# Transposing the mixer input before its scale and shift are known, and scaling it in place

## The chip, the cores and the metric

One core of one Trainium2 chip. The metric is the device time of one execution in microseconds (us); a kernel's time is the median of several executions. TensorE (PE), VectorE (DVE), ScalarE (ACT) and GpSimd (POOL) compute; SP, ACT and POOL issue DMA transfers, each on a queue of its own (in the profile q1 is SP's, q10 ACT's, q0 POOL's).

## The reference, cut to what matters

One trunk layer of width 2048 over 128 context tokens and 512 latent tokens. A modulation vector per token group comes from a matrix product with the conditioning vectors; its first two parts shift and scale the normalised input of the mixer:

```python
xs = x_sample + grid_pos_embed(x_sample.shape[1], x_sample.dtype)[None]
mod = (silu(cond) @ w_mod + b_mod)            # six parts of 2048: sh1, sc1, gt1, sh2, sc2, gt2
h = rmsnorm(x, norm_mix) * (1 + sc1) + sh1    # both groups, each with its own sh1, sc1
proj = h @ w_in                               # q, k, v first
qkv = silu(short_conv(qkv, conv_w))
```

After this come a DeltaNet scan, a gated MLP, the merge, the output projection and a retrieval over 16384 experts. Everything is float32.

## The kernel before, in words

The work around the change is at the start of the program, in three blocks. A block ends when all five engines have reached its end, and one follows the other (`build`, L2713 to L2718).

**`modulation` (L428).** SP loads 32 tiles of `w_mod` of 1 MB each into a ring of four slots (L451; `load_tile`, L232, waits until the tile four places earlier has been used), and behind them the first four `w_qkv` tiles. PE multiplies each tile by the conditioning vectors (`modulate`, L246); four tiles make one of eight groups. ACT copies a group's result out of PSUM (`copy`, L476), and PE turns it into columns (`turn`, L504). Between these, PE forms the row part of the positions (`encode`, L513, behind every third tile from 4 to 25), DVE adds it and the column part to the four latent blocks x[1] to x[4] (L550 to L555), ACT takes the sum of squares of each block (L489), DVE the reciprocal root and five normalised blocks (L561). The normalised blocks 1 to 4 have buffers of their own; x[1] to x[4] hold the sums of input and position, which ACT writes to DRAM (`x_rows`, four transfers of 1 MB, L498) behind the copy of group 6, for use much later. At the end DVE makes `shift1` and `scale1` (L565 to L570).

**`mixer_input` (L574).** For each of 16 slices of 128 features PE transposes five 128x128 squares (L604), DVE scales and shifts the latent 512 columns (L585) and ACT the context's 128 (L593), each out of PSUM into `l.h` and `c.h`. POOL issues the first three `w_mod` tiles of the next stage (`mod_load`, L285), and DVE waits for `x_rows` (L587), since the memory of x[1] to x[4] is written next.

**`qkv` for the context (L613).** 24 tiles of `w_qkv`: PE projects (`project`, L239, 16 products of 128x128x128 each), DVE convolves (L729 to L735), ACT applies SiLU and a square (L804, L807), PE sums the squares of tile n-1 behind the projection of tile n (`norm_sum`, L660), and behind every tile PE does one more `w_mod` tile (`mod_tile`, L254), whose loads POOL issues (`mod_feed`, L297). SP first loads `w_gates` and `c_masks` (1.4 MB together, L636, L638), then `w_qkv` tiles from the fifth on, each when the ring slot four places back is free.

Of the kernel before, what the change touches and what calls it, by code (L numbers as in the profile page):

```python
# [9 lines left out]
ACT = mybir.ActivationFunctionType  # L10
# [63 lines left out]
def after(e, sem, n):  # L74

    if n > 0:
        e.wait_ge(sem, n)
# [350 lines left out]
def modulation(nc, t, a):  # L428
# [5 lines left out]
    normed = x[0:1] + [t.m[:, o:o + D] for o in (DD + D, DD + 2 * D, DD + 3 * D, E + D)]  # L434
    t.normed = normed
    row_enc = t.m[0:2, BG:BG + (NB - 1) * D // 2].rearrange("p (b n) -> p b n", b=NB - 1)
# [9 lines left out]
    with nc.Block() as block:  # L446
# [10 lines left out]
        def _(act):  # L457
# [36 lines left out]
            for n in range(NB, groups):  # L494
                copy(n)
                if n == groups - 2:
                    for b in range(1, NB):
                        act.dma_start(t.x_rows[b], x[b]).then_inc(t.x_spilled, 16)  # L498
# [4 lines left out]
        def _(pe):  # L503
# [9 lines left out]
            def encode(i):  # L513
# [3 lines left out]
                else:  # L517
                    pe.wait_ge(row_read, i)
                pe.matmul(t.ps[:, 3, :], which, row_enc[:, i // 2, i % 2 * COL:(i % 2 + 1) * COL],
                          start=True, stop=True).then_inc(row_ps, 1)  # L520

            pe.wait_ge(small_done, 2)
            pe.wait_ge(sel_step, 3)
            for n in range(groups):

                after(pe, copied, n - 1)
                for kq in range(4):
                    tile_full(pe, t, 4 * n + kq)
                    mm = modulate(pe, t.ps[:, n % 2, :], t, 4 * kq, tile_slot(t, 4 * n + kq), kq == 0, kq == 3)
                    mm.then_inc(t.tile_done, 1)  # L530
                    if 4 <= 4 * n + kq < 28 and (4 * n + kq) % 3 == 1:
                        encode((4 * n + kq) // 3 - 1)
                if n:
                    turn(n - 1)
# [3 lines left out]
        def _(dve):  # L538
# [22 lines left out]
            for b in range(NB):  # L561
                nc.vector.tensor_scalar(normed[b], x[b], inv[:, b:b + 1], None, ALU.mult).then_inc(xn_done, 1)
            dve.wait_ge(turned, groups)
            dve.wait_ge(t.x_in, 16 * 8)
            for i, out in ((0, t.shift1), (1, t.scale1)):  # L565
# [4 lines left out]
                                           op0=ALU.add, op1=ALU.mult).then_inc(t.init, 1)  # L570
    t.tiles += tiles


def mixer_input(nc, t, a):  # L574

    c, l = t.group[:2]
    x = t.normed
    turned, lat_read, ctx_read = (t.sem("mi_" + n) for n in ("turned", "lat_read", "ctx_read"))
    with nc.Block() as block:  # L579
        @block.vector  # L580
        def _(dve):
            for k in range(KD):

                dve.wait_ge(turned, k + 1)
                nc.vector.tensor_scalar(l.h[:, k, :], t.ps[:, 2 * (k % 4), :], t.scale1[:, k, 1:2], t.shift1[:, k, 1:2],  # L585
                                        ALU.mult, ALU.add).then_inc(lat_read, 1)
            dve.wait_ge(t.x_spilled, 16 * (NB - 1))  # L587

        @block.scalar
        def _(act):  # L590
            for k in range(KD):
                act.wait_ge(turned, k + 1)
                nc.scalar.activation(c.h[:, k, :], t.ps[:, 2 * (k % 4) + 1, 0:P], ACT.Identity,  # L593
                                     bias=t.shift1[:, k, 0:1], scale=t.scale1[:, k, 0:1]).then_inc(ctx_read, 1)

        @block.tensor
        def _(pe):
            for k in range(KD):

                after(pe, lat_read, k - 3)  # L600
                after(pe, ctx_read, k - 3)
                for b in range(NB):
                    out = t.ps[:, 2 * (k % 4), (b - 1) * P:b * P] if b else t.ps[:, 2 * (k % 4) + 1, 0:P]
                    mm = pe.transpose(out, x[b][:, k * P:(k + 1) * P], t.ident[:])  # L604
                mm.then_inc(turned, 1)

        @block.gpsimd
        def _(pool):
            for m in range(3):
                mod_load(pool, t, a, m)  # L610


def qkv(nc, t, a, g, block):  # L613
# [13 lines left out]
                                   "qk_done", "gates_ps", "gates"))  # L627
    first_staged = t.sem("qk_first_staged")
    tiles, normed = 3 * H, 2 * H
# [30 lines left out]
    def _(pe):  # L660
# [39 lines left out]
        for n in range(tiles):  # L700

            after(pe, psum_read, n - 3)
            tile_full(pe, t, n)
            project(pe, t.ps[:, n % 4, 0:nt], tile_slot(t, n), h).then_inc(t.tile_done, 1)
            if 1 <= n <= normed:
# [15 lines left out]
    def _(dve):  # L721
# [23 lines left out]
        def last_product():  # L745

            dve.wait_ge(gates, 9)
            nc.vector.tensor_tensor(beg, beg, beta, ALU.mult).then_inc(gates, 1)

        for n in range(tiles):  # L750
            conv(n)
# [31 lines left out]
    def _(act):  # L783
# [12 lines left out]
        for n in range(tiles):  # L796
# [5 lines left out]
            if n < normed:  # L802
                after(act, qk_done, n - 1)
                nc.scalar.activation(s[n % 2], y[n % 2], ACT.Silu).then_inc(silu_done, 1)  # L804
                act.wait_ge(silu_done, n + 1)
                after(act, norm_ps, n)
                nc.scalar.activation(sq, s[n % 2], ACT.Square).then_inc(sq_done, 1)  # L807
            else:
                nc.scalar.activation(heads[:, n, :], y[n % 2], ACT.Silu).then_inc(silu_done, 1)
            gelu_rows(act, nc, t, behind[n])  # L810
            if n == q + 6 and not ctx:
# [1884 lines left out]
def build(nc, a):  # L2696
    with ExitStack() as ctx:
# [16 lines left out]
        retire()  # L2714
        mixer_input(nc, t, a)
        retire()
        with nc.Block() as block:
# [140 lines left out]
```

## Time and profile before

| what | us |
|---|---|
| median of three executions | 4789.78 |
| lowest and highest of them | 4781.29, 4797.11 |
| profiled execution, first to last instruction (its span) | 4786.7 |
| end of `modulation`, first transpose of `mixer_input` | 111.7, 111.84 |
| first product of the context's projection | 130.30 |

Of the profiled execution the span is what is known of its own time; it lies 3.1 us under the median of the three. Times in the rows below count from the first instruction. A row of the timeline has start, busy time, engine, line, operation, output<-input, shape and count, and in brackets the engine's idle time before it and what ended that. A row of the windows has, for a stretch, its length, the busy time of each engine with its count of instructions in brackets, then the granted share of TensorE's clock, the busy share of the 16 DMA engines and the GB/s they moved.

### The profile page before, as it was taken

What the parts mean: (1) busy time and instruction counts of PE and PEld (TensorE: products, weight loads), DVE (VectorE), ACT (ScalarE), POOL (GpSimd) and SP (SyncE); (2) the same over time, 40 slices, a digit from 0 to 9 for tenths busy, and PEclk for the clock granted to TensorE, in tenths of its full rate; (3) what the DMA queues carried; (4) which work ended last, traced back from release to release, by engine and by line L of the source; (5) the groups of instructions that cost most, each with busy time, mean ns of one, the idle gap of its engine ahead of it and who ended that gap; (6) DMA issues with size and microseconds to landing.
All of it is one profiled execution on the core that took longest, in us unless ns stands there. A gap on an engine that the chain in (4) does not pass through costs nothing.

```text
span 4786.7 us, 61495 instructions
## 1 busy us (share of the span) xinstructions
PE 4559.0 (95%) x25813; PEld 3365.2 (70%) x25813; DVE 3043.3 (64%) x4399; ACT 579.6 (12%) x1080; POOL 1656.3 (35%) x1110
## 2 busy tenths in 40 slices
PE   6989999999888999899999998999999999999997
PEld 2776346444888544347555545699999999999997
DVE  1451006888877777417777667988865557886556
ACT  1531001441222100000000001110000000000000
POOL 0131001674655554210544443433432332322221
PEclk8999999999999999999999999999999999999998
DMA  9919898997322998997999997579999999999998
GB/s 400 383 63 368 314 347 321 384 393 288 110 83 90 361 390 352 421 369 270 408 420 420 411 413 300 220 294 420 418 417 421 405 406 419 417 417 419 404 420 326
DMA packets 237328, 1663.47 MB, mean 348 GB/s; under 512 B 28231, under 2 KB 32729, under 8 KB 37787
## 3 DMA queue, kind: packets, MB, share of 16 engines
q0 software_dynamic: 130048, 939.72, 48.6%
q1 hardware_dynamic: 98884, 673.84, 35.6%
q10 hardware_dynamic: 8120, 45.98, 2.4%
q8 instruction: 204, 3.34, 0.3%
q14 instruction: 72, 0.58, 0.0%
HBM read 1639.68 MB, written 18.94 MB: 347 GB/s over the span
## 4 chain that ended last, share of the span: by engine, by line
PE 43%; DVE 6%; DMA 5%; issue 1%; POOL 1%; ACT 0%; ACTq 0%; DVEq 0%; POOLq 0%
PE ps L242 25%; PE ps L2415 14%; DMA arena_sb<-peer_v,arena_sb 4%; DVE arena_sb L401 2%; PE ps L2357 1%; PE ps L1815 1%; DMA arena_sb<-peer_u,arena_sb 1%; POOL arena_sb L350 1%; DMA x_rows<-arena_sb 0%; DVE arena_sb L2117 0%; DVE arena_sb L2107 0%; DVE arena_sb L2109 0%; DVE arena_sb L2190 0%; DMA arena_sb<-w_query 0%; DVE arena_sb L2114 0%
## 5 line engine op out<-in xcount | busy, mean ns | idle before, releaser
L242 PE MATMUL ps<-arena_sb 128*128 128x224 f32 (+3 forms) x9728 | 2292.2, 396 | 10.7 <-PEq L579 6.2
L242 PEld LDWEIGHTS ps<-arena_sb 128*128 128x128 f32 x9728 | 1669.6, 191 | 627.2 <-issue 335.0
L401 DVE SCALAR_TENSOR_TENSOR arena_sb<-arena_sb 128x2048 f32<-128x2048 f32 x412 | 988.7, 2400 | 460.8 <-DMA arena_sb<-peer_v,arena_sb 431.3
L396 DVE CUSTOM_DVE_ANT_0 arena_sb<-arena_sb 128x2048 f32<-128x2048 f32 x416 | 977.7, 2366 | 306.5 <-DMA arena_sb<-peer_u,arena_sb 305.8
L350 POOL DMA_INDIRECT arena_sb<-peer_v,arena_sb x416 | 617.6, 1485 | 1147.9 <-DVE arena_sb L401 918.4
L350 POOL DMA_INDIRECT arena_sb<-peer_u,arena_sb x416 | 642.2, 1544 | 811.2 <-DVE arena_sb L396 462.4
L2415 PE MATMUL ps<-arena_sb 128*128 128x224 f32 x4096 | 776.3, 352 | 1.3 <-ACT arena_sb L2454 0.6
L2415 PEld LDWEIGHTS ps<-arena_sb 128*128 128x128 f32 x4096 | 774.4, 190 | 1.9 <-issue 1.0
L1625 PE MATMUL ps<-arena_sb 128*128 128x512 f32 x768 | 342.8, 603 | 25.3 <-DMA arena_sb<-w_gb_r 10.2
L1625 PEld LDWEIGHTS ps<-arena_sb 128*128 128x128 f32 x768 | 145.6, 193 | 217.7 <-issue 197.0
L1815 PE MATMUL ps<-arena_sb 128*128 128x512 f32 x640 | 277.7, 596 | 4.4 <-DMA arena_sb<-w_out 2.2
L288 POOL DMA_DIRECT2D arena_sb<-w_mod x64 | 34.8, 544 | 590.8 <-PE ps L249 478.0
L1815 PEld LDWEIGHTS ps<-arena_sb 128*128 128x128 f32 x640 | 121.8, 191 | 159.5 <-issue 153.6
L927 POOL TENSOR_TENSOR arena_sb<-arena_sb 128x1024 f32<-128x1024 f32 x60 | 159.8, 2682 | 185.6 <-ACT arena_sb L1206 175.6
L1682 DVE TENSOR_TENSOR arena_sb<-ps,arena_sb 128x512 f32<-128x512 f32 x16 | 11.1, 692 | 288.9 <-PE ps L1625 288.9
L249 PE MATMUL ps<-arena_sb,scond_sb 128*32 128x512 f32 x768 | 128.4, 703 | 33.0 <-DMA arena_sb<-w_mod 33.0
L1340 PE MATMUL ps<-arena_sb 128*128 128x512 f32 x320 | 138.4, 593 | 0.8 <-DMA arena_sb<-w_vg 0.4
L1010 PE MATMUL ps<-arena_sb 128*64 128x32 f32 (+1 forms) x3520 | 122.9, 228 | 5.0 <-ACT arena_sb L1215 2.5
L1010 PEld LDWEIGHTS ps<-arena_sb 128*64 128x64 f32 x3520 | 114.0, 143 | 11.4 <-ACT arena_sb L1215 6.1
L2604 DVE TENSOR_SCALAR arena_sb<-arena_sb 128x128 f32<-128x128 f32 x448 | 119.7, 353 | 0.0
L1340 PEld LDWEIGHTS ps<-arena_sb 128*128 128x128 f32 x320 | 60.5, 190 | 78.1 <-issue 75.8
L2454 ACT ACTIVATE arena_sb<-ps 128x224 f32<-128x224 f32 (+27 forms) x107 | 28.9, 270 | 676.9 <-PE ps L242 676.9
(288 smaller groups left out, 2983.7 us busy)
## 6 DMA issues: line engine op xcount, KB each, us to landing
arena_sb<-peer_ut SPq DMA_DIRECT2D x128, 1024.0 KB, 9.3
arena_sb<-peer_vt SPq DMA_DIRECT2D x128, 1024.0 KB, 9.2
arena_sb<-w_mod POOLq DMA_DIRECT2D x64, 1024.0 KB, 9.2
arena_sb<-w_qkv SPq DMA_DIRECT2D x48, 1024.0 KB, 9.2
arena_sb<-w_out SPq DMA_DIRECT2D x48, 1024.0 KB, 7.4
arena_sb<-w_query SPq DMA_DIRECT2D x48, 1024.0 KB, 6.9
arena_sb<-w_mod SPq DMA_DIRECT2D x32, 1024.0 KB, 8.8
arena_sb<-w_ga_r SPq DMA_DIRECT2D x32, 1024.0 KB, 7.8
```

What stands on the lines that cost most here:

```text
L242: mm = pe.matmul(out, weights[:, k * P:(k + 1) * P], x[:, k, :], start=(k == 0), stop=(k == chunks - 1))
L249: mm = pe.matmul(out[32 * j:32 * j + 32, :], t.scond[:, k + j, :], weights[:, j * COL:(j + 1) * COL], start=start, stop=stop, tile_positio ...
L350: nc.gpsimd.indirect_dma_start(slot, None, a["peer_v" if adds else "peer_u"], bass.IndirectOffsetOnAxis(ap=seg.index[:, p:p + 1], axis=0)) ...
L396: nc.vector.tensor_tensor_reduce(rows, rows, total, 1.0, 0.0, ALU.mult, ALU.add, seg.dots[:, p:p + 1]).then_inc(t.rows_used, 1)
L401: nc.vector.scalar_tensor_tensor(out=total, in0=rows, scalar=seg.weight[:, p:p + 1], in1=total, op0=ALU.mult, op1=ALU.add).then_inc(t.rows ...
L927: nc.gpsimd.tensor_tensor(lev[:, k % 2], mt, over(nmask[:, 1 - r, k], H), ALU.mult).then_inc(s["level_masked"], 1)
L1010: mm = pe.matmul(compact(bank(2 + u), k, side)[rows, h % 4, a], lhs[:, h, rows], changed(rhs, k, second)[:, h, a], start=True, stop=True, ...
L1340: mm = pe.matmul(t.ps[:, 4 * c + b, :], h[:, k, b * P:(b + 1) * P], tile_slot(t, H + 4 * c + kq)[:, kk * COL:(kk + 1) * COL], start=(k == ...
L1625: mm = pe.matmul(t.ps[:, s, :], x[:, k, :], tile_slot(t, n)[:, kk * COL:(kk + 1) * COL], start=(k == 0), stop=(k == 4 * tiles - 1))
L1815: mm = pe.matmul(t.ps[:, 4 * (c % 2) + b, :], merged[:, k, b * P:(b + 1) * P], tile_slot(t, 4 * c + kq)[:, kk * COL:(kk + 1) * COL], start ...
L2415: mm = pe.matmul(t.ps[:, bank_of[h][first + i], 0:DENSE], ring[slot_of[n - 1]][:, col:col + P], acts[:, s, :], start=(s == 0 and h == 0), ...
L2604: nc.vector.tensor_scalar(weighted[i][:, u], t.pick_iota, key1[:, e:e + 1], weight[:, e:e + 1], ALU.is_equal, ALU.mult)
```

## The change

`mixer_input` is gone. PE transposes the normalised blocks within `modulation`, two or three slices behind each of the tiles 24 to 30; ACT copies the latent part and DVE the context's part out of PSUM, unscaled. `encode` moves to the tiles 13 to 20. `x_rows` is written behind the copy of group 7 instead of group 6, behind the 16 latent copies in ACT's order. POOL's three `mod_load` are issued within `modulation`, once 29 tiles are done. In `qkv` for the context DVE scales `c.h` in place, slice by slice, ahead of its loop and waits there for `x_rows`; the first projection follows it slice by slice. ACT scales `l.h` in place, one slice behind each of the first 16 tiles, and waits for `x_rows` ahead of the 17th.

```diff
@@ modulation, ACT
             for n in range(NB, groups):
                 copy(n)
-                if n == groups - 2:
+                for k in range(8 * (n - NB), min(8 * (n - NB) + 8, KD)):
+                    act.wait_ge(input_turned, k + 1)
+                    nc.scalar.activation(l.h[:, k, :], t.ps[:, 4 + k % 2, :], ACT.Copy).then_inc(lat_kept, 1)
+                if n == groups - 1:
                     for b in range(1, NB):
                         act.dma_start(t.x_rows[b], x[b]).then_inc(t.x_spilled, 16)
@@ modulation, PE
+            def turn_input(k):
+                pe.wait_ge(xn_done, NB)
+                after(pe, lat_kept, k - 1)
+                after(pe, ctx_kept, k - 1)
+                for b in range(NB):
+                    out = t.ps[:, 4 + k % 2, (b - 1) * P:b * P] if b else t.ps[:, 6 + k % 2, 0:P]
+                    mm = pe.transpose(out, normed[b][:, k * P:(k + 1) * P], t.ident[:])
+                mm.then_inc(input_turned, 1)
...
-                    if 4 <= 4 * n + kq < 28 and (4 * n + kq) % 3 == 1:
-                        encode((4 * n + kq) // 3 - 1)
-                if n:
+                    if 13 <= 4 * n + kq < 21:
+                        encode(4 * n + kq - 13)
+                    for k in turns_at.get(4 * n + kq, ()):
+                        turn_input(k)
+                    if n == groups - 1 and kq == 1:
+                        turn(n - 1)
+                if 0 < n < groups - 1:
                     turn(n - 1)
@@ modulation, DVE
+            for k in range(KD):
+                dve.wait_ge(input_turned, k + 1)
+                nc.vector.tensor_copy(c.h[:, k, :], t.ps[:, 6 + k % 2, 0:P]).then_inc(ctx_kept, 1)
@@ modulation, POOL (the rest of mixer_input is removed)
+            pool.wait_ge(row_read, 2 * (NB - 1))
+            pool.wait_ge(x_done, NB - 1)
+            pool.wait_ge(t.tile_done, tiles - 3)
             for m in range(3):
                 mod_load(pool, t, a, m)
@@ qkv, PE
+            if ctx and n == 0:
+                for k in range(KD):
+                    pe.wait_ge(scaled, k + 1)
+                    mm = pe.matmul(t.ps[:, 0, 0:nt], tile_slot(t, 0)[:, k * P:(k + 1) * P], h[:, k, :], start=(k == 0),
+                                   stop=(k == KD - 1))
+                mm.then_inc(t.tile_done, 1)
+            else:
+                project(pe, t.ps[:, n % 4, 0:nt], tile_slot(t, n), h).then_inc(t.tile_done, 1)
@@ qkv, DVE
+        if ctx:
+            for k in range(KD):
+                nc.vector.tensor_scalar(h[:, k, :], h[:, k, :], t.scale1[:, k, 0:1], t.shift1[:, k, 0:1], ALU.mult,
+                                        ALU.add).then_inc(scaled, 1)
+            dve.wait_ge(t.x_spilled, 16 * (NB - 1))
@@ qkv, ACT
+                if ctx and n == normed:
+                    act.wait_ge(t.x_spilled, 16 * (NB - 1))
                 nc.scalar.activation(heads[:, n, :], y[n % 2], ACT.Silu).then_inc(silu_done, 1)
+            if ctx and n < KD:
+                rows = t.group[1].h[:, n, :]
+                nc.scalar.activation(rows, rows, ACT.Identity, bias=t.shift1[:, n, 1:2], scale=t.scale1[:, n, 1:2])
```

Here `turns_at` gives tiles 24 to 27 two slices each, 28 and 29 three, 30 two.

## Rows read from the trace of the kernel before

**Rows 1.** The page: its first line, the span.

```profile
span 4786.7 us, 61495 instructions
```

**Rows 2.** Windows of the first stage: length, engines, clock, DMA share, GB/s.

```profile
60.00:87.00 27.00, 22.94 (x118) 7.58 (x118) 5.02 (x6) 5.20 (x6) 0.00 (x0) 0.75 1.01 422
...
112.00:127.00 15.00, 12.05 (x80) 11.03 (x79) 11.95 (x16) 7.33 (x16) 1.81 (x3) 0.83 1.01 425
127.00:130.00 3.00, 0.00 (x0) 0.00 (x0) 0.00 (x0) 0.00 (x0) 0.00 (x0) 0.57 0.24 101
```

**Rows 3.** Timeline from the last modulation tile to the third projected tile.

```profile
106.19 1.27 PE L249 MATMUL ps<-arena_sb,scond_sb 128*32 128x512 f32 x8 [2.33 <-DMA arena_sb<-w_mod]
...
111.84 12.21 PE L604 MATMUL ps<-ident_sb,arena_sb 128*128 128x128 f32 x80 [0.87 <-PEq L446]
...
113.35 1.81 POOL L288 DMA_DIRECT2D arena_sb<-w_mod  x3 [112.90 <-issue]
...
117.39 8.71 DVE L585 TENSOR_SCALAR arena_sb<-ps,scale_sb,shift_sb 128x512 f32<-128x512 f32 x12 [0.20 <-PE ps L604]
...
130.30 5.69 PE L242 MATMUL ps<-arena_sb 128*128 128x128 f32 x32 [6.25 <-PEq L579]
...
136.03 0.35 DVE L729 TENSOR_SCALAR arena_sb<-ps,cw_sb 128x128 f32<-128x128 f32 x1 [9.92 <-PE ps L242]
...
136.91 3.84 PE L242 MATMUL ps<-arena_sb 128*128 128x128 f32 x32
...
141.90 3.84 PE L242 MATMUL ps<-arena_sb 128*128 128x128 f32 x32
```

**Rows 4.** Ends of the first two blocks (lines L446 and L579): duration ns, start.

```profile
L446 DVEq DRAIN  x1: 225/225/225, 111.3 to 111.3; - x1
...
L579 POOLq DRAIN  x1: 15800/15800/15800, 114.2 to 114.2; - x1
```

**Rows 5.** Timeline: tiles 20 to 22, the last `encode`, the five normalised blocks.

```profile
74.92 5.12 PE L249 MATMUL ps<-arena_sb,scond_sb 128*32 128x512 f32 x24
...
89.25 1.41 PE L519 MATMUL ps<-arena_sb 2*128 2x512 f32 x2
...
96.65 6.07 DVE L562 TENSOR_SCALAR arena_sb<-arena_sb,stat_sb 128x2048 f32<-128x2048 f32 x5
```

**Rows 6.** Windows: transposes alone on PE, at the lower and at a rising clock.

```profile
112.00:116.00 4.00, 4.00 (x20) 4.00 (x20) 2.30 (x3) 1.37 (x3) 1.81 (x3) 0.50 1.03 428
116.00:120.00 4.00, 4.00 (x33) 4.00 (x32) 3.54 (x6) 2.72 (x6) 0.00 (x0) 0.85 1.00 420
```

**Rows 7.** Timeline: a modulation tile and a `turn` at either clock.

```profile
39.12 1.93 PE L249 MATMUL ps<-arena_sb,scond_sb 128*32 128x512 f32 x8 [3.07 <-DMA arena_sb<-w_mod]
...
51.56 1.05 PE L509 MATMUL ps<-sel_sb,arena_sb 128*128 128x2 f32 x8
...
83.72 1.87 PE L509 MATMUL ps<-sel_sb,arena_sb 128*128 128x2 f32 x8
...
90.58 1.07 PE L249 MATMUL ps<-arena_sb,scond_sb 128*32 128x512 f32 x8
```

**Rows 8.** DMA queues of 105 to 110 us: packets, MB, share of 16 engines.

```profile
q10 hardware_dynamic: 148, 1.08, 51.2%
q1 hardware_dynamic: 147, 1.07, 50.8%
```

**Rows 9.** DMA queues of 115 to 120 us: packets, MB, share of 16 engines.

```profile
q0 software_dynamic: 72, 0.59, 27.9%
q10 hardware_dynamic: 52, 0.29, 14.6%
```

**Rows 10.** Prices: a page row, a timeline row, and ACT's share of 160 to 180 us.

```profile
L2604 DVE TENSOR_SCALAR arena_sb<-arena_sb 128x128 f32<-128x128 f32 x448 | 119.7, 353 | 0.0
...
269.08 0.63 ACT L1198 ACTIVATE arena_sb<-arena_sb 128x512 f32<-128x512 f32 x1 [1.19 <-DVE arena_sb L1105]
...
160.00:180.00 20.00, 20.00 (x166) 15.58 (x165) 9.72 (x21) 14.33 (x21) 3.14 (x6) 1.00 1.01 414
```

More of the change, by code:

```diff
@@ L434, in modulation @@
     normed = x[0:1] + [t.m[:, o:o + D] for o in (DD + D, DD + 2 * D, DD + 3 * D, E + D)]
-    t.normed = normed
+    c, l = t.group[:2]
+    turns_at = {24: range(0, 2), 25: range(2, 4), 26: range(4, 6), 27: range(6, 8), 28: range(8, 11), 29: range(11, 14),
+                30: range(14, 16)}
+    lat_kept, ctx_kept, input_turned = (t.sem("mo_" + n) for n in ("lat_kept", "ctx_kept", "input_turned"))
     row_enc = t.m[0:2, BG:BG + (NB - 1) * D // 2].rearrange("p (b n) -> p b n", b=NB - 1)
@@ L570, in _ @@
                                            op0=ALU.add, op1=ALU.mult).then_inc(t.init, 1)
[L571 to L605, printed above, removed]
         @block.gpsimd
         def _(pool):
+            pool.wait_ge(row_read, 2 * (NB - 1))
+            pool.wait_ge(x_done, NB - 1)
+            pool.wait_ge(t.tile_done, tiles - 3)
             for m in range(3):
                 mod_load(pool, t, a, m)
+    t.tiles += tiles
 def qkv(nc, t, a, g, block):
@@ L627, in qkv @@
                                    "qk_done", "gates_ps", "gates"))
-    first_staged = t.sem("qk_first_staged")
+    first_staged, scaled = t.sem("qk_first_staged"), t.sem("qk_scaled")
     tiles, normed = 3 * H, 2 * H
@@ L703, in _ @@
             tile_full(pe, t, n)
-            project(pe, t.ps[:, n % 4, 0:nt], tile_slot(t, n), h).then_inc(t.tile_done, 1)
+            if ctx and n == 0:
[6 more added lines that the diff above has]
+                project(pe, t.ps[:, n % 4, 0:nt], tile_slot(t, n), h).then_inc(t.tile_done, 1)
             if 1 <= n <= normed:
@@ L2714, in build @@
         retire()
-        mixer_input(nc, t, a)
-        retire()
         with nc.Block() as block:
```

## The prediction

> **What bounds the kernel now.** The change touches the first 260 us of a span of 4786.7 us [rows 1]; whatever it wins or loses there is carried to the end, since the blocks behind follow one another. So I read that stretch only, first by windows. From 60 to 87 us, and again from 112 to 127 us, the 16 DMA engines are busy throughout and move 422 to 425 GB/s [rows 2]: a tile of 1 MB (1.0486 MB) costs 2.5 us of the machine whoever asks for it. The stage is bound by transfers, not by PE. Then from 127 to 130 us nothing computes and the transfers run dry [rows 2]: that is the gap to explain.
>
> The timeline shows its two sides: the last modulation tile at 106.19, 80 transposes from 111.84 to 124.05, DVE's last scaling until 126.10, and the first product of the projection only at 130.30 [rows 3]. The instructions at the block's end tell who was late: POOL's DRAIN starts at 114.2, takes 15.8 us and so ends at 130.0 [rows 4]. POOL had done nothing in this block but issue three `w_mod` transfers at 113.35 to 115.16 [rows 3]; its DRAIN ends when they have landed. Neither the transposes nor `x_rows` set the 130.30. From there PE runs without a gap, one projected tile every 4.99 us (136.91 to 141.90 [rows 3]), with DVE's first convolution at 136.03.
>
> **What the change does to the parts.**
>
> *Earlier normalised blocks.* The last `encode` moves from behind tile 25 to behind tile 20. Before, it ended at 90.66 and the last normalised block at 102.72, 12.1 us later [rows 5]. Tiles 20 to 22 start at 74.92 and take 1.7 us each [rows 5]; with tile 20 done at about 76.6 and `encode` another 1.4 us, the blocks are ready at about 78 + 12 = 90.
>
> *PE from 90 us.* It has tiles 25 to 31, 16 slices of five transposes, and two `turn`. A tile is 1.07 us at the upper clock and 1.93 at the lower, a `turn` 1.05 and 1.87 [rows 7]; five transposes are 1.0 us at the lower clock (20 in 4 us) and about 0.6 at a granted 0.85 (33 in 4 us) [rows 6]. All at the upper clock: 7 x 1.07 + 16 x 0.6 + 2 x 1.05 = 19.2 us; all at the lower: 7 x 1.93 + 16 x 1.0 + 2 x 1.87 = 33.2 us. The 80 transposes of before took 12.2 us [rows 3], 1.27 of the 9.6 at the upper clock, because the clock rose within them; I take the same factor: 24 us, so tile 31 ends at about 114 (109 to 123), against 107.5 before. The copies out of PSUM lie beside it: 0.6 us of ACT and at most 0.35 us of DVE a slice; without that cover PE would wait, since only two slices fit.
>
> *The three `w_mod` of POOL.* Tile 28 is done after 4 tiles, 8 slices and one `turn` of that work, (4.3 + 4.8 + 1.05) x 1.27 = 13 us, at 103; the first bytes come about 4 us after the issue (issued 113.35; 0.59 MB on q0 between 115 and 120 us, at half the machine 2.8 us of flow [rows 9]), so at 107, ten microseconds earlier than before.
>
> *`x_rows`.* It was issued in front of all this; it is now issued behind tile 31 and a copy, at about 115, and flows from about 117.5. This transfer of four tiles is the heart of the sum, since DVE waits for it ahead of the first convolution; behind DVE stand ACT's SiLU and square, and PE, which stops at the first `norm_sum`, behind the second projected tile. How fast does it flow? When two queues have work each gets half (51.2 and 50.8% [rows 8]). A stretch with three full queues isn't in the trace; the one slice where all three appear has q0 and q10 each filling a part only (27.9 and 14.6% [rows 9]). Bounds: a half, as with two, and nothing better than a third, as equal turns would give. I take the third, the same rule with one more taker.
>
> The Trainium skill ("DMA: Bandwidth & Descriptors", queues, rings and completion order) says each DMA engine goes round the queues that have work, a packet at a time. By that the third holds, and the transfer called last gets no precedence for being waited for; no run here shows three full queues yet.
>
> *Adding up.* From 107 to 117.5 q1 (`w_qkv` 0 to 3) and q0 share: 10.5 us / 2.5 = 4.2 tiles, 2.1 each, which leaves q0 0.9, q1 1.9, `x_rows` 4. Thirds until q0 is through: 0.9 x 3 x 2.5 = 6.8 us, 124.3; before, the DRAIN ended 2.5 us after the transfers thinned out (127.5 to 130.0 [rows 2, 4]), so POOL holds the block's end until about 127. That is only 3 us better than 130, since POOL's wait has moved and not gone. Halves then: q1's last 1.0 until 129.3, `x_rows` 2.1 left; `w_gates` and `c_masks` (1.3 tiles) until 136, and 0.8 left; `w_qkv` 4 takes half of the rest: 140. With the landing, DVE starts its convolution at about 139 to 141 (134 if PE ran at the upper clock), against 136.03. PE meanwhile has projected two tiles and done one `mod_tile` (before: one tile and that). From the convolution to `norm_sum`: three times 0.35 on DVE and two short ACT steps, 2 us; `mod_tile` 1.07; so the third tile starts at 142 to 144 instead of 141.90, or at 138 with the upper clock. Shift: 0 to +2 in the likeliest case, down to -4, up to +6.
>
> *What is hidden.* DVE's 16 scalings of `c.h` run ahead of the first projection: 0.35 us each by the nearest row [rows 10], 5.6 in all, as long as the first tile at the lower clock (5.69 [rows 3]); added: one slice, 0.35. ACT's 16 scalings of `l.h`: 0.63 us each [rows 10] in a stage where ACT is busy 14.3 of 20 us [rows 10], that is 3.6 of 4.99 a tile: they fit, at nothing. If `Identity` called for a table load, 1.3 more per tile, ACT would need 5.5 of 4.99, 0.5 x 16 = 8 us; no row shows an `Identity` between a square and a root, but the 16 of `mixer_input` ran behind an exponential without one. The removed block's ends, latent scaling and the second DRAIN are in the sum above, and SP's order is unchanged. Transfers stay ahead of PE behind the third tile: the fifth `w_qkv` is needed ten microseconds after it.
>
> The sum: 4786.7 + 1 = 4788 for the profiled execution; the median shown lies 3.1 above it, within its own spread. Predicted: 4790 us. About 0.3%, 14 us, is what a measurement of this kernel can tell from no change, and the whole gap to be won, from 115 (POOL and DVE both through) to 130, is 15.
>
> **Rivals.** *A, `x_rows` in time (chance 0.22).* If the clock is up from 90 us, or `x_rows` gets more than a third, only POOL's DRAIN counts: the projection starts at 123 to 125 instead of 130.3 and is not stopped: -7, 4783. For: the transposes stood dense and rose to 0.85 within 8 us [rows 6]. Against: the bytes. Everything that was moved by 127.5 before has to be moved by then again, and `x_rows` is now last.
>
> *B, the clock stays low (0.07), slower than before.* One mechanism: PE at the granted 0.5 from the `encode` tiles on. Tiles 13 to 20 would cost about 4 us each with their `encode` (1.93 [rows 7], and about 2, an estimate from the 1.41 of [rows 5], where the clock rose), above the 2.5 of the transfers, so the blocks come at about 104 instead of 90; then 33 us more to 137, `x_rows` alone on the machine 3 + 10 us, convolution at 153, third tile at 160: +18 to +20, 4808. It decides where PE's pace passes 2.5 us a tile and the clock doesn't follow. For: the mean granted clock is 0.75 from 60 to 87 us [rows 2]. Against: that stretch is full of waits for tiles, and 0.5 went to 0.85 as PE was kept busy [rows 6].
>
> *C, thirds for longer (0.10).* `x_rows` shares with q0 for a second time, since `mod_feed`'s fourth tile is issued behind PE's first `mod_tile`: half a tile more each, 3 to 8 us: 4797.
>
> *D, nothing hidden (0.01):* the transposes wait for tiles as before and the change only reorders; no shift, within the forecast.
>
> **How the numbers follow.** The forecast has 0.60. Forecast, A and C all lie within 14 us, with the spread of the executions (8 us either way) taking some of A and of C over the bound. Faster by over 0.3%: 0.08, out of A and chance; slower: 0.08, B and a little of C; same: 0.84. The range takes in A less half the spread, and C: 4776 to 4803; B and the tails, under 2 in 10, are left out.
>
> **What would show it.** Right: a DRAIN of POOL at the end of `modulation` until 124 to 128; two projected tiles, then PE idle for `norm_sum` and DVE for `x_rows` until 134 to 141; the third tile at 138 to 144. Wrong: a first convolution before 128, or a block end before 120 (then faster), or a lower clock from 60 to 115 us (then slower).

## The result, and the profile after

The changed kernel is 0.2% slower: 4800.7 us against 4790.6 (medians of 20 runs each), a ratio of 1.0018 with a 95% interval of [1.0011, 1.0025], so +8.6 us (5 to 12). That is inside the predicted range (4776 to 4803) and inside 0.3%, but the step that was forecast, about +1 us, is outside the interval. The profiled span went from 4786.7 [rows 1] to:

```profile
span 4795.3 us, 61523 instructions
```

First the windows, for before those stretches that were not shown yet. The columns are those of [rows 2]: busy time of PE, PEld, DVE, ACT and POOL, the granted clock, the DMA share, GB/s.

```profile
60.00:92.00 32.00, 27.59 (x136) 8.43 (x136) 6.33 (x8) 5.20 (x6) 0.00 (x0) 0.75 1.01 418
92.00:112.00 20.00, 12.93 (x65) 6.75 (x66) 7.42 (x11) 6.56 (x9) 0.00 (x0) 0.70 0.99 399
...
127.00:140.00 13.00, 9.70 (x67) 8.77 (x68) 1.05 (x3) 3.18 (x4) 0.53 (x1) 0.74 0.58 214
140.00:200.00 60.00, 60.00 (x497) 47.32 (x497) 28.48 (x62) 42.96 (x63) 8.94 (x17) 1.00 1.00 402
0.00:200.00 200.00, 156.35 (x978) 90.11 (x979) 59.65 (x110) 72.55 (x107) 11.48 (x25) 0.89 0.97 389
0.00:300.00 300.00, 239.05 (x1888) 157.93 (x1890) 103.99 (x207) 106.94 (x162) 42.58 (x53) 0.90 0.83 330
```

The same of the changed kernel:

```profile
60.00:92.00 32.00, 30.89 (x98) 8.70 (x102) 9.37 (x11) 9.23 (x10) 0.00 (x0) 0.52 0.76 282
92.00:112.00 20.00, 14.28 (x104) 8.43 (x100) 8.76 (x15) 7.47 (x14) 0.00 (x0) 0.83 0.80 313
112.00:127.00 15.00, 10.87 (x88) 6.66 (x80) 2.81 (x11) 6.90 (x12) 1.81 (x3) 0.97 1.01 399
127.00:140.00 13.00, 3.37 (x16) 3.40 (x17) 3.87 (x16) 1.28 (x1) 0.00 (x0) 0.51 1.01 418
140.00:200.00 60.00, 57.93 (x465) 45.93 (x464) 25.35 (x57) 44.41 (x65) 7.88 (x15) 0.97 0.98 396
0.00:200.00 200.00, 149.96 (x895) 80.17 (x896) 52.07 (x116) 74.01 (x106) 9.90 (x22) 0.86 0.93 370
0.00:300.00 300.00, 235.85 (x1658) 149.54 (x1659) 93.10 (x211) 117.40 (x174) 33.30 (x49) 0.89 0.83 330
```

Read the last two columns. From 60 to 112 us the transfers, full before, run at 0.76 and 0.80 of the engines' time: 282 and 313 GB/s against 418 and 399, that is 15.3 MB against 21.4. At the 402 GB/s that the kernel before moves from 140 to 200 us, at a share of 1.00, 6.1 MB are 15 us. From 112 to 140 us it is the other way: before has its gap (214 GB/s), the changed kernel is full throughout and moves 11.4 MB against 9.2, which wins 5.6 us back. At 200 us the changed kernel is 3.8 MB behind (370 against 389 GB/s times 200 us), 9.5 us at 402 GB/s. By 300 us both have moved the same (330).

The timeline of the changed kernel, in the order of [rows 5] and then [rows 3], says why:

```profile
71.28 1.94 PE L249 MATMUL ps<-arena_sb,scond_sb 128*32 128x512 f32 x8
...
73.14 2.07 PE L525 MATMUL ps<-arena_sb 2*128 2x512 f32 x2
...
94.61 6.07 DVE L582 TENSOR_SCALAR arena_sb<-arena_sb,stat_sb 128x2048 f32<-128x2048 f32 x5
100.73 2.40 PE L535 MATMUL ps<-ident_sb,arena_sb 128*128 128x128 f32 x10 [5.72 <-DVE arena_sb L582]
...
121.13 1.06 PE L249 MATMUL ps<-arena_sb,scond_sb 128*32 128x512 f32 x8
...
122.27 1.89 ACTq L504 DMA_DIRECT2D x_rows<-arena_sb  x4
...
136.13 4.19 DVE L752 TENSOR_SCALAR arena_sb<-arena_sb,scale_sb,shift_sb 128x128 f32<-128x128 f32 x16 [11.62 <-PEq L449]
136.63 5.33 PE L700 MATMUL ps<-arena_sb 128*128 128x128 f32 x32 [12.66 <-DVE arena_sb L752]
...
142.89 3.84 PE L242 MATMUL ps<-arena_sb 128*128 128x128 f32 x32
...
146.94 0.35 DVE L729 TENSOR_SCALAR arena_sb<-ps,cw_sb 128x128 f32<-128x128 f32 x1 [6.61 <-DMA x_rows<-arena_sb]
...
148.65 0.80 ACT L819 ACTIVATE arena_sb<-arena_sb,shift_sb,scale_sb 128x512 f32<-128x512 f32 x1
...
150.30 5.34 PE L242 MATMUL ps<-arena_sb 128*128 128x128 f32 x32
```

At the lower clock (1.2 GHz) a modulation tile takes 1.94 us and its `encode` 2.07. Starts one tile apart, 71.28 to 75.15, are 3.87 us, against the 2.5 us in which a tile can be moved; SP's loads wait for PE to free one of the four slots (29.9 us in 8 waits, the longest 6.5 us, from 60 to 92 us), and the transfers fall to 0.76. PE was busy 30.89 of these 32 us at a mean granted clock of 0.52. The hole from 92 to 112 us has a second cause, which the row at 100.73 shows: behind tile 24 the program has PE transpose first, and PE stands for 5.72 us until the normalised blocks are there, and uses no tiles meanwhile. So the normalised blocks end at 100.7, only 2 us earlier than before (102.7 [rows 5]), tile 31 ends at 122.2 instead of 107.5, and the steps behind it are late with it. The block's end (line L449 of the changed kernel, to hold against [rows 4]; duration in ns, then the start):

```profile
L449 POOLq DRAIN  x1: 21396/21396/21396, 114.5 to 114.5; - x1
...
L449 DVEq DRAIN  x1: 225/225/225, 124.3 to 124.3; - x1
```

Everybody else is through at 124.5; POOL's DRAIN holds the block until 135.9. As a mark for the end of the context projection I use the first product of the next stage, for before and then for the changed kernel (timeline rows): 10.1 us later.

```profile
263.07 3.76 PE L982 MATMUL ps<-tri_sb,gate_rows_sb 128*128 128x128 f32 x16 [5.27 <-PEq L2717]
```

```profile
273.20 3.52 PE L992 MATMUL ps<-tri_sb,gate_rows_sb 128*128 128x128 f32 x16 [5.50 <-PEq L2725]
```

This mark is the local measure of all experiments: behind it the profiled executions take anything from 4512.1 us (e11_spread_again) to 4538.3 (e10_warm_two), more than any shift looked for here. Medians are given beside it. The mark itself differs between two executions of one program by 1.6 us (e1 and e11 below) and 4.1 us (e8 and e12).

### The profile page after: what moved, and what is told of

The parts are those of the page before. It is cut to its first block, busy times and chain, and to the rows that moved or that the text cites. A ratio compares the mean times of both kernels' runs of the same rounds, so it can differ in the third digit from the quotient of the medians.

```text
span 4795.3 us, 61523 instructions
## 1 busy us (share of the span) xinstructions
PE 4565.1 (95%) x25813; PEld 3366.5 (70%) x25813; DVE 3034.3 (63%) x4415; ACT 592.5 (12%) x1096; POOL 1648.1 (34%) x1110
## 4 chain that ended last, share of the span: by engine, by line
PE 35%; DMA 11%; DVE 7%; issue 1%; POOL 1%; ACT 0%; ACTq 0%; DVEq 0%; POOLq 0%
PE ps L242 24%; DMA arena_sb<-peer_v,arena_sb 11%; PE ps L2425 8%; DVE arena_sb L401 3%; PE ps L1825 1%; PE ps L2367 1%; POOL arena_sb L350 1%; DMA x_rows<-arena_sb 0%; DVE arena_sb L2127 0%; DVE arena_sb L2117 0%; DVE arena_sb L2119 0%; DVE arena_sb L2200 0%; DVE arena_sb L2124 0%; DVE arena_sb L2114 0%; DVE arena_sb L2155 0%
## 5 line engine op out<-in xcount | busy, mean ns | idle before, releaser
L1825 PEld LDWEIGHTS ps<-arena_sb 128*128 128x128 f32 x640 | 120.9, 190 | 159.9 <-issue 150.8
L1350 PEld LDWEIGHTS ps<-arena_sb 128*128 128x128 f32 x320 | 60.4, 190 | 79.6 <-issue 74.7
```

Source lines behind the costliest of these rows:

```text
L1350: mm = pe.matmul(t.ps[:, 4 * c + b, :], h[:, k, b * P:(b + 1) * P], tile_slot(t, H + 4 * c + kq)[:, kk * COL:(kk + 1) * COL], start=(k == ...
L1825: mm = pe.matmul(t.ps[:, 4 * (c % 2) + b, :], merged[:, k, b * P:(b + 1) * P], tile_slot(t, 4 * c + kq)[:, kk * COL:(kk + 1) * COL], start ...
```

## The experiments

Three causes stood against each other at first: the pace of PE in the packed tiles, the place of the `x_rows` writes, and POOL's DRAIN at the block's end. The first four kernels take these apart.

**Encodings spread out (e1_spread).** The changed kernel, with an `encode` behind every odd tile from 5 to 19.

```
-                    if 13 <= 4 * n + kq < 21:
-                        encode(4 * n + kq - 13)
+                    if 5 <= 4 * n + kq < 21 and kq % 2:
+                        encode((4 * n + kq - 5) // 2)
```

> One part changed against the changed kernel (span 4795.3, third projected tile at 150.3, normalised blocks complete at 100.7): the eight position products stand behind every second tile from 5 to 19 instead of behind each tile from 13 to 20. Theory 1 (PE's pace at the lower clock in the packed stretch makes the blocks late and starves the transfers): blocks complete at 86 to 90, tile 31 done near 110 instead of 122, third tile at 141 to 144, span 4786 to 4789. Theory 2 (the write of x_rows as the last transfer sets the third tile wherever PE stands): the blocks come earlier but the third tile moves by less than 3, span 4792 or more.

Measured: 4781.5 us against 4793.4, ratio 0.998 [0.9965, 0.9994]: 0.2% below before. The normalised blocks are complete at 88.9 us, as expected, and the third projected tile starts at 139.44, earlier than expected. The mark is at 261.05, 12.1 us ahead of the changed kernel. Windows:

```profile
60.00:92.00 32.00, 29.26 (x132) 9.96 (x128) 11.80 (x15) 8.47 (x11) 0.00 (x0) 0.61 0.97 380
...
112.00:127.00 15.00, 0.15 (x1) 0.18 (x2) 0.67 (x4) 1.98 (x3) 0.00 (x0) 0.53 1.01 413
```

The transfers are back at 0.97 although the clock is up for little of the time (0.61): two tiles and one `encode` take 3.64 + 2.07 us at the lower clock, little more than the 5.0 of two transfers. And look at 112 to 127 us: PE does nothing, the DMA engines are full. POOL's DRAIN even grew to 24.1 us. It costs PE 15 us, and the stage still ends earlier than in either kernel before it.

**`x_rows` early (e2_rows_early).** The four writes behind the square root instead of behind the last copy.

```
             nc.scalar.activation(root, root, ACT.Sqrt).then_inc(rstd, 1)
+            for b in range(1, NB):
+                act.dma_start(t.x_rows[b], x[b]).then_inc(t.x_spilled, 16)
...
-                if n == groups - 1:
-                    for b in range(1, NB):
-                        act.dma_start(t.x_rows[b], x[b]).then_inc(t.x_spilled, 16)
```

> One part changed against the changed kernel: x_rows is issued behind the root of the sums of squares, at about 94, instead of behind the copy of group 7, at 122. Theory 1 (PE's pace): blocks still at 100.7 and tile 31 still at 122 or later, so the third tile moves only by what POOL's end gains from sharing with one queue less, 2 to 5 us, span 4790 to 4793. Theory 2 (x_rows last): block end at 128 to 131 instead of 136, the first convolution straight behind the first product, third tile at 139 to 143, span 4784 to 4788.

Measured: 4800.5 us against 4793.4, ratio 1.0007 [0.9994, 1.002]; mark at 271.15. The writes had landed at 120.9 and no convolution waited for them, yet the third tile started at 149.75, 0.6 us earlier, and the mark came only 2.1 us earlier than in the changed kernel. Part of that is this execution: from 60 to 92 us, where the two programs are the same, it moved 259 GB/s and the changed kernel 282, which is 1.8 us.

**POOL's loads in the next block (e3_pool_next).** The three `mod_load` of the modulation block are POOL's first work in the projection's block.

```
-            for m in range(3):
-                mod_load(pool, t, a, m)
...
+        if ctx:
+            for m in range(3):
+                mod_load(pool, t, a, m)
```

> One part changed against the changed kernel: the three w_mod loads of POOL are issued first thing in the context's projection block, instead of within modulation. Theory 3 (the end of modulation, held by POOL until 136.0, costs the time): block end at 125 to 127, first product at 126 to 127, and the third tile at 143 to 146, span 4788 to 4791. Theory 2 (x_rows): the block ends early too, but PE stops at the first sum of squares until x_rows has landed, 140 to 146; third tile earlier by less than 4, span 4791 or more.

Measured: 4804.0 us against 4793.4, ratio 1.0022 [1.0012, 1.0031]; mark at 281.51, worst of all. The first product starts at 130.2, 6.4 us ahead of the changed kernel, and nothing is won: what was not moved while the block ran has to be moved later, and `x_rows` lands at 155.4. The third tile, which both theories had expected earlier, came 9.6 us later (159.88).

**A warmer PE (e4_warm).** Four products of the identity by itself ahead of each of the tiles 8 to 24, to keep the clock up while the encodings stay packed.

```
+                    if 8 <= 4 * n + kq < 25:
+                        for _ in range(4):
+                            pe.matmul(t.ps[:, 2, 256:384], t.ident[:], t.ident[:], start=True, stop=True)
```

> Added to the changed kernel: four products of 128x128 by 128 columns ahead of each of the tiles 8 to 24, into an unused part of a PSUM bank, results not read. It tests the clock alone. Theory 1 with the clock as the cause: PE is granted the upper level from about 50 to 92 us, where it had 0.5, a packed tile takes 2.6 us instead of 4.0 in spite of the added work, and the blocks complete at 88 to 93; span 4786 to 4791. If the clock isn't the cause: the granted level stays at 0.5, a packed tile takes about 4.8 us, blocks at 107 or later, span 4800 or more.

Measured: 4794.1 us against 4793.4, ratio 1.0003 [0.9989, 1.0016]; mark at 271.77. Timeline of three operations of a packed tile:

```profile
77.56 1.12 PE L525 MATMUL ps<-arena_sb 2*128 2x512 f32 x2
78.61 1.16 PE L546 MATMUL ps<-ident_sb 128*128 128x128 f32 x8
79.70 1.07 PE L249 MATMUL ps<-arena_sb,scond_sb 128*32 128x512 f32 x8
```

The clock did rise (0.84 from 60 to 92 us), tile and `encode` then take 2.2 us together; but my four products cost 1.16, so a tile still starts every 3.1 us. The last `encode` ends no earlier than in the changed kernel, the blocks are ready at 101.0 (I had expected 88 to 93), and little was won.

These four suggested one account for all: up to the end of the context projection every kernel moves the same bytes (330 GB/s over 300 us in all of them), the transfers are nearly full in the end (0.96 to 1.00 from 140 to 200 us), and so only the transfer time left unused on the way counts, whoever left it. The next four kernels test that.

**Packed and spread in the kernel before (e5_before_packed, e6_before_spread).** The input is still transposed behind the block; only the place of `encode` is changed, to behind tiles 13 to 20 as in the change, or behind the odd tiles as in e1_spread.

```
-                    if 4 <= 4 * n + kq < 28 and (4 * n + kq) % 3 == 1:
-                        encode((4 * n + kq) // 3 - 1)
+                    if 13 <= 4 * n + kq < 21:
+                        encode(4 * n + kq - 13)
```

```
-                    if 4 <= 4 * n + kq < 28 and (4 * n + kq) % 3 == 1:
-                        encode((4 * n + kq) // 3 - 1)
+                    if 5 <= 4 * n + kq < 21 and kq % 2:
+                        encode((4 * n + kq - 5) // 2)
```

> The kernel before with the eight position encodings behind tiles 13 to 20 instead of every third tile; the input is still transposed after the block. Theory now (the stretch to the end of the context projection is bound by its DMA bytes; whatever DMA time a slow TensorE leaves unused early is lost): the packed tiles take 3.9 us at the 0.5 clock as in the changed kernel, DMA share of 60 to 92 us falls from 1.01 to about 0.76, some 8 us are lost, the context projection ends 5 to 9 us later than 263.0 and the median is about 6 us up. Rival (packing costs only because the transposes of the input stand behind it): context end within 2 us of 263.0, median unchanged.

> The kernel before with the encodings behind the odd tiles 5 to 19. Theory now (DMA bytes): DMA was already at 1.01 from 60 to 92 us in the kernel before, so nothing is to be had from it; the idle 0.42 of 127 to 140 us stays; context end within 2 us of 263.0, median within 2 us of before. Rival (the spread is itself what makes e1_spread faster, whatever is done with the transposes): blocks 10 us earlier, modulation end and context end 4 us or more earlier, median 6 to 10 us down as in e1_spread.

Measured: packed 4803.1 us against 4788.2, ratio 1.0036 [1.0022, 1.0049], mark at 276.06 (+13.0); spread 4797.2, 1.0021 [1.0007, 1.0034], mark at 265.07 (+2.0). Windows of the packed one:

```profile
60.00:92.00 32.00, 31.23 (x94) 8.65 (x90) 8.84 (x12) 7.80 (x9) 0.00 (x0) 0.50 0.72 268
...
140.00:160.00 20.00, 17.82 (x127) 14.97 (x128) 4.69 (x12) 7.95 (x11) 1.05 (x2) 0.80 0.70 254
```

and one of the spread one:

```profile
127.00:140.00 13.00, 8.11 (x50) 7.18 (x51) 2.52 (x6) 2.13 (x4) 0.53 (x1) 0.74 0.54 195
```

Packing alone costs 13 us, more than I had expected (5 to 9): from 60 to 92 us alone it moved 4.8 MB less than before, 12 us, where I had expected 8. The gap behind the block is still there, as in the kernel before, only later (0.70 from 140 to 160 us). Spreading alone leaves that gap (0.54) and gains nothing. With e1_spread this is a table of two by two by the mark, one execution each: moving the transposes is worth 2.9 us under packed encodings (276.06 to 273.20) and 4.0 us under spread ones (265.07 to 261.05), packing costs 11 to 12 us under either.

**The block's end without POOL (e7_spread_sp) and a wait of its own for the first write (e8_spread_split).** Both are e1_spread with one wait less in its chain. In the first SP issues the three loads between its tiles of `w_qkv`, on semaphores of their own; in the second VectorE waits for one `x_rows` write only, ahead of the first normalisation, and ScalarE for the other three later.

```
                 load_tile(sp, t, a["w_qkv"], tiles + n, n)
+                if n == 0:
+                    sp.wait_ge(row_read, 2 * (NB - 1))
+                    sp.wait_ge(x_done, NB - 1)
+                if n < 3:
+                    mod_load(sp, t, a, n)
```

```
-            dve.wait_ge(t.x_spilled, 16 * (NB - 1))
...
+                if n == 1:
+                    dve.wait_ge(t.x_first, 16)
                 if 1 <= n <= normed:
                     normalise(n - 1)
```

> The changed kernel with the encodings behind odd tiles (as e1_spread) and the three modulation loads issued by SP between the first tiles of w_qkv, so that POOL has nothing to drain. Theory now (DMA bytes): the block ends near 112 us instead of 126.2, the products start some 14 us earlier, but DMA was already at 1.0 from 112 to 240 us in e1_spread, so the same bytes end at the same time: context end within 3 us of 260.9, median within 3 us of e1_spread's. Rival (the DRAIN of POOL and the x_rows writes behind it hold the chain): third projected tile some 8 us earlier than 139.4, context end 252 to 255, median 6 to 9 us below e1_spread's.

> As e1_spread, with a semaphore of its own for the first write of x_rows: VectorE waits for that one alone ahead of the first normalisation, ScalarE for the other three ahead of the last third of the tiles. Theory now (DMA bytes): the first convolution is not held to the last landing (136.1 us in e1_spread) any more and starts near 131, but DMA is full throughout: context end within 2 us of 260.9, median within 3 us of e1_spread's. Rival (the wait for x_rows sets the pace): everything behind it moves up by its 5 us, context end near 256, median 5 us below e1_spread's.

Measured: e7_spread_sp 4788.0 us against 4788.2, ratio 1.0007 [0.9994, 1.002], mark at 259.00; e8_spread_split 4787.3, 1.0003 [0.9991, 1.0015], mark at 255.88. In e7_spread_sp the first product stands at

```profile
110.61 5.97 PE L697 MATMUL ps<-arena_sb 128*128 128x128 f32 x32 [2.54 <-DVE arena_sb L749]
```

26 us ahead of the changed kernel's, and the mark moved 2 us against e1_spread. Even these 2 us may not be the edit's: from 60 to 92 us, where it changes nothing yet, this execution moved 420 GB/s against 380, 3 us. Behind its second projected tile PE stood until `x_rows` had landed and the first squares were there:

```profile
134.06 0.80 PE L657 MATMUL ps<-arena_sb,ones_sb 128*128 128x128 f32 x2 [12.71 <-ACT arena_sb L809]
```

The mark of e8_spread_split looked like the rival's (256); but there the early tiles themselves had run better, 422 GB/s from 60 to 92 us against 380 in e1_spread under the same code up to there, and the second execution below, with 420 GB/s there, did not repeat it (260.01).

**The parts together, two repeats, and a lighter warm-up.** e9_best has the edits of e1, e7 and e8; e11 and e12 are e1 and e8 again; e10_warm_two is the changed kernel with two identity products ahead of tiles 13 to 21 only.

```
+                    if 13 <= 4 * n + kq < 22:
+                        for _ in range(2):
+                            pe.matmul(t.ps[:, 2, 256:384], t.ident[:], t.ident[:], start=True, stop=True)
```

> Spread encodings, modulation loads by SP and the separate wait for the first write of x_rows, together. By the account of bytes (every kernel so far has moved 99.1 MB when its context projection ends; at 200 us before had moved 77.8 MB, the changed kernel 74.0, e8_spread_split 81.0, and the shift of the context end is the difference at 0.404 MB a us): DMA full from 60 to 240 us, some 81 MB at 200 us, context end 255 to 258; median 4 to 8 us below before. Rival (what is gained there is taken back by later blocks): context end the same, median within 2 us of before.

> The changed kernel, encodings still packed behind tiles 13 to 20, with two products of the identity by itself (128 by 128, 0.29 us each in e4_warm at the upper clock) ahead of tiles 13 to 21. Theory (the lower clock is what makes a packed tile cost 3.9 us): where the clock is granted at 1.0 a packed tile takes about 1.07 + 1.12 + 0.58 = 2.8 us, the blocks are ready near 92 instead of 100.7, DMA moves some 75.5 to 77 MB by 200 us instead of 74.0, context end 265 to 269. Rival (the number of packed products sets the pace, whatever the clock; or two products don't raise the clock): the blocks at 100 or later, context end at 272 or later.

> e1_spread once more, beside e9_best and e12_split_again on one chip, in more rounds: its median was 9 us below before although its context end was only 2 us earlier. By the account of bytes it should stand 1 to 4 us below before and 3 to 5 above e12_split_again; the rival (the gain of e1_spread comes from behind the context projection) keeps it 8 to 10 us below before.

> e8_spread_split once more: its context end was 7 us earlier than before's but its median equal to before's. By the account of bytes its median should be 4 to 7 us below before. Rival (later blocks take it back): within 2 us of before.

Measured, against 4790.9 us of before: e9_best 4784.7 (0.9985 [0.9972, 0.9998]), e10_warm_two 4797.2 (1.0012 [0.9998, 1.0025]), e11_spread_again 4780.3 (0.9983 [0.997, 0.9995]), e12_split_again 4787.0 (0.9988 [0.9974, 1.0001]). Timeline of a packed tile in e10_warm_two, at the upper clock (2.4 GHz):

```profile
78.66 0.71 PE L546 MATMUL ps<-ident_sb 128*128 128x128 f32 x4
79.31 1.07 PE L249 MATMUL ps<-arena_sb,scond_sb 128*32 128x512 f32 x8
80.30 1.12 PE L525 MATMUL ps<-arena_sb 2*128 2x512 f32 x2
```

2.9 us in all, 0.71 of them the added work. The blocks are ready at 97.1 (I expected 92; 100.7 in the changed kernel), and the mark is at 268.48, within the 265 to 269 of the clock theory. Four executions with packed encodings and nothing between them were granted 0.50 to 0.52 from 60 to 92 us (the changed kernel, e2, e3, e5), the two with identity products 0.84 and 0.89. In e9_best the first product comes at 114.35 and the first convolution at 120.9, the earliest convolution of all, and then PE waits:

```profile
127.00:140.00 13.00, 9.91 (x84) 7.85 (x83) 5.49 (x12) 9.48 (x15) 2.19 (x4) 1.00 1.01 425
140.00:160.00 20.00, 11.73 (x76) 10.73 (x76) 2.38 (x7) 6.96 (x10) 0.53 (x1) 0.74 0.92 373
```

and in its timeline, the fifth tile:

```profile
148.27 6.64 PE L243 MATMUL ps<-arena_sb 128*128 128x128 f32 x32 [9.41 <-DMA arena_sb<-w_qkv]
```

PE is busy 11.7 of 20 us for lack of tiles. An early start buys nothing where the bytes aren't there. The mark is at 262.29; I had expected 255 to 258 from the 81 MB of e8_spread_split, and this execution had 78.2.

**The account, over all kernels.** MB at 200 us are the GB/s of the window 0 to 200 times 200 us; the third column is what these are short of before's 77.8, at 402 GB/s; the fourth is the mark minus before's 263.07.

| kernel | MB at 200 us | shift by bytes, us | shift of the mark, us |
|---|---|---|---|
| changed kernel | 74.0 | +9.5 | +10.1 |
| e1_spread | 79.0 | -3.0 | -2.0 |
| e2_rows_early | 74.8 | +7.5 | +8.1 |
| e3_pool_next | 70.6 | +17.9 | +18.4 |
| e4_warm | 74.6 | +8.0 | +8.7 |
| e5_before_packed | 72.8 | +12.4 | +13.0 |
| e6_before_spread | 77.0 | +2.0 | +2.0 |
| e7_spread_sp | 79.6 | -4.5 | -4.1 |
| e8_spread_split | 81.0 | -8.0 | -7.2 |
| e9_best | 78.2 | -1.0 | -0.8 |
| e10_warm_two | 75.8 | +5.0 | +5.4 |
| e11_spread_again | 79.4 | -4.0 | -3.6 |
| e12_split_again | 79.2 | -3.5 | -3.1 |

Thirteen executions, whose first products start anywhere from 110.6 (e7_spread_sp) to 142.2 us (e5_before_packed), agree with the bytes to 1 us. The mark of one execution is still no median: e8_spread_split and e12_split_again are one program and differ by 4.1 us.

**How far the account reaches.** The agreement in the table is less of a proof than it looks. From the third projected tile on (in e9_best from the fifth) PE runs the projection in every kernel without a wait for a transfer: in before it is busy 60.00 of 60.00 us from 140 to 200, a tile takes 4.99 us [rows 3], and it is SP's loads that wait for PE to free their slots, 73.3 us in all from 160 to 240 us. So a late third tile makes the bytes at 200 us late as well, whatever made it late. The third tile indeed tells the mark as well as the bytes do: its shift against before's 141.90 agrees with the mark's to 0.6 us in ten of the thirteen kernels, to 1.2 in e7_spread_sp and to 1.7 in the changed kernel (+8.4). Only e9_best, whose third tile comes 15.1 us early and where PE then stops for the fourth and fifth tile, breaks this.

That the transfers place the third tile rests on other evidence: on the runs that took one wait away and moved it little or the wrong way (e2_rows_early, e3_pool_next, e7_spread_sp), on the stop in e9_best, and on the bytes counted earlier. At 140 us, before most of the projection, they already give the shift of the mark to 2.2 us in eleven of the thirteen kernels; in the other two, e5_before_packed (6.6 us for 13.0) and e3_pool_next (15.0 for 18.4), transfer time is still left unused behind 140 us (shares of 0.70 from 140 to 160 and 0.91 from 160 to 180 us).

**What stays open.** The medians follow the mark only roughly. e1_spread stands below before by 0.20% and, as e11_spread_again, 0.17%, 8 to 10 us, of which its marks explain 2 to 4. e7_spread_sp and e8_spread_split, with earlier marks, stand at before's time, not within 3 us of e1_spread's as I had expected; e6_before_spread stands 0.21% above with a mark of +2.0, where I had expected 2 us at most. Of the last four, e9_best (6 us below, expected 4 to 8) fits the account, e12_split_again (3.9, expected 4 to 7) nearly, and e11_spread_again fits its rival. The intervals are some 6 us wide to either side, so part of this is chance; whether later blocks add to it was not settled. The best version measured is e1_spread, below before with both intervals under 1, while the changed kernel's lies above 1.

## Why the prediction was right or wrong

**What bounds the stage: right, and then only half used.** The prediction read [rows 2] as "a tile of 1 MB (1.0486 MB) costs 2.5 us of the machine whoever asks for it. The stage is bound by transfers, not by PE." Its sum then followed the starts of operations (DRAIN, `x_rows`, first convolution, third tile) and read the shift off the third tile. As a measure that was sound: the third tile came 8.4 us late (150.30 against 141.90), the mark 10.1, and the two agree in every kernel but e9_best. What the sum has no term for is transfer time left unused before 112 us, which has to be made up later whatever wait is taken away: 15 us here. "The whole gap to be won, from 115 ... to 130, is 15" was wrong for the same reason. In that gap most of the transfer time was in use; only 5.6 us of it was to be had, and the change did win those.

**Earlier normalised blocks: the step that failed.** "With tile 20 done at about 76.6 ... the blocks are ready at about 78 + 12 = 90." They were ready at 100.7. The 76.6 is the pace of before, where one tile in three has an `encode` behind it; eight in a row run at 3.87 us a tile at the lower clock. The rest followed from there: tile 31 ended at 122.2 instead of 114, the first convolution came at 146.94 instead of 139 to 141, the third tile at 150.30 instead of 142 to 144. e5_before_packed shows that this alone, without any other part of the change, costs the transfers from 60 to 92 us (268 GB/s against 418), and e1_spread and e10_warm_two that either more distance or a higher clock gives the time back, in whole or in part (380 and 329 GB/s, against 282 in the changed kernel).

**Rival B was the mechanism, at 0.07.** It priced a packed tile at "about 4 us", the blocks at "about 104" and a shift of +18 to +20. Tile (3.87) and blocks (100.7) were nearly right. I put it aside since "0.5 went to 0.85 as PE was kept busy" [rows 6]; that was said of transposes, and under modulation tiles and encodings PE was busy 30.89 of 32 us at 0.52. The Trainium skill ("TensorE: Matmul & The Clock Gate", Part 1) says that activity releases the lower clock; here it stayed low through nearly unbroken work, and rose while identity products stood between (0.84 in e4_warm, 0.89 in e10_warm_two). The shift was smaller than B's because the clock came back behind the encodings (0.83 from 92, 0.97 from 112 us), where B had 33 us at the lower one, and because the removed gap gave 5.6 us. That the time lies in the predicted range is in part luck: B was left out of the range at 4808 and came out at about half its price, and the upper end of 4803 stood there for C. The signs were clearer than the number. A lower clock between 60 and 115 us was named as a sign of a slower kernel, and it came (0.52 from 60 to 92); the DRAIN until 135.9, the convolution at 146.94 and the third tile at 150.30 all lie outside what was named for a right prediction.

**PE from the blocks to tile 31.** Predicted 24 us (19.2 to 33.2); from 100.7 to 122.2 it took 21.5: right, nearer to the upper clock's bound.

**POOL's three loads and the DRAIN.** "POOL's wait has moved and not gone" was right: 135.9 against 130.0, where I had put it at 127 from the earlier blocks. Its price was wrong: with the DMA full beneath it, e7_spread_sp took it away and the mark came 2 us earlier, no more than two executions of one program differ by.

**`x_rows` in thirds.** Right where three queues had work, and now in a row. DMA queues of the changed kernel, 127.5 to 130 us:

```profile
q0 software_dynamic: 46, 0.37, 34.8%
q1 hardware_dynamic: 42, 0.34, 33.8%
q10 hardware_dynamic: 43, 0.35, 33.2%
```

This agrees with the rule of the Trainium skill ("DMA: Bandwidth & Descriptors", queues, rings and completion order) as the prediction drew on it. The wait came where it was expected too, ahead of the first convolution (146.94, predicted 139 to 141, late by the blocks). But "the heart of the sum" it was not: e2_rows_early took the wait away and won 2.1 us, perhaps 4 without the slower start of that execution.

**What is hidden.** The scalings lay where they were put: `c.h` 16 in 4.19 us (0.26 each, I had 0.35) with a first product of 5.33, `l.h` 0.80 us each (I had 0.63). PE runs without a gap from 160 to 200 us in both kernels, and no table load came with `Identity`.

**Rivals A and C.** A (clock up, projection at 123 to 125, 4783) did not happen in the changed kernel; e7_spread_sp produced its early start and not its gain. C's second sharing of `x_rows` was not looked for; the late blocks and the won gap give the size of the shift without it.

## What to carry to other kernels

Where the transfers are full at the end of a stage, keep the account in bytes: here the end moved by the transfer time that was left unused on the way, whichever engine left it, and an earlier start or a shorter wait was worth only as much of such a hole as it filled. Take the bytes early, before the stage settles into its steady pace; later they only repeat the result. Before packing small work of PE behind consecutive tiles, add its time at the lower clock to the tile's, also at the lower clock, and hold the sum against the tile's transfer; if it is longer, spread the work over more tiles.

## What the runs showed of the hardware that was not expected

PE, busy 30.89 of 32 us with modulation tiles and encodings, was granted 0.52 on average; in the same code spread over twice as many tiles two executions got 0.61 and 0.66 (e1, e11), and kernels with the same code up to there 0.80 and 0.68 (e8, e12). So the clock under such work differs between executions. What is moved from 60 to 92 us differs too (380 to 422 GB/s, 1.3 MB or 3 us), though not by this clock alone: 381 at 0.66 in e11, 420 at 0.68 in e12. POOL's DRAIN at the block's end took 15.8 us before, 21.4 in the changed kernel and 24.1 in e1_spread, and 41 ns in e7_spread_sp, where POOL had loaded nothing.
